# Index heads of a two-block transformer kernel: the two 128-column score products become one 256-column product, and half of the read-out moves from ScalarE to VectorE

## The reference, cut to what matters

```python
s_idx = relu(einsum('bqhd,bkd->bqhk', q_idx, k_idx) * IDX_DIM ** -0.5)   # 8 heads, IDX_DIM 64
score = einsum('bqhk,bqh->bqk', s_idx, w)           # w = w_idx * 8 ** -0.5
score = where(causal, score, -1e30)
_, sel = top_k(score, topk)                         # topk = 64 of 256 keys
```

## Time and profile before

| quantity | value |
|---|---|
| median of the runs | 1114.24 us |
| the profiled execution's own time | 1114.35 us |
| its span, first to last instruction | 1112.5 us |
| busy, TensorE / weight loads | 1106.8 us (99%) / 941.2 us (85%) |
| busy, VectorE / ScalarE / GpSimd | 790.6 us (71%) / 621.2 us (56%) / 58.0 us (5%) |
| mean granted clock of TensorE | 1.000 |

### The profile page before, as it was taken

One profiled execution on the slowest core, in us unless ns is written; L12 is line 12 of the kernel. 1 busy time (PEld: TensorE's weight loads), 2 busy tenths in 40 slices (PEclk: granted clock), 3 DMA queues, 4 the chain that ended last, 5 costly groups with the idle time before them and its releaser, 6 DMA issues.

```text
span 1112.5 us, 14865 instructions
## 1 busy us (share of the span) xinstructions
PE 1106.8 (99%) x5830; PEld 941.2 (85%) x5830; DVE 790.6 (71%) x1136; ACT 621.2 (56%) x825; POOL 58.0 (5%) x105
## 2 busy tenths in 40 slices
PE   9999999999999999999999999999999999999998
PEld 8888888888888888888888888888877788888887
DVE  6777754667987677775477787557898786777752
ACT  6556542677656456554356556337787854656530
POOL 1000000100000000000000000011343000000000
PEclk9999999999999999999999999999999999999999
DMA  9755565654454665555565555557643455555541
GB/s 317 252 190 189 189 246 190 211 162 141 165 195 157 203 189 190 189 189 189 191 206 190 189 189 189 189 154 255 224 150 122 149 181 164 191 188 194 192 179 38
DMA packets 142581, 208.02 MB, mean 187 GB/s; under 512 B 9296, under 2 KB 100584, under 8 KB 142512
## 3 DMA queue, kind: packets, MB, share of 16 engines
q1 hardware_dynamic: 139408, 198.07, 52.7%
q0 software_dynamic: 3088, 9.00, 2.4%
q10 hardware_dynamic: 16, 0.00, 0.0%
HBM read 205.98 MB, written 2.65 MB: 188 GB/s over the span
## 4 chain that ended last, share of the span: by engine, by line
PE 98%; ACT 1%; DMA 0%; issue 0%; DVE 0%; SPq 0%; ACTq 0%; DVEq 0%
PE banks L1810 28%; PE banks L1696 16%; PE banks L1698 16%; PE banks L1697 16%; PE banks L1807 14%; PE banks L1768 1%; PE banks L2046 1%; PE banks L1718 1%; PE banks L1983 1%; DMA raw<-in_ffn_w_gate 0%; PE banks L2076 0%; PE banks L2073 0%; PE banks L2142 0%; PE banks L2016 0%; PE banks L2019 0%
## 5 line engine op out<-in xcount | busy, mean ns | idle before, releaser
L1143 DVE TENSOR_TENSOR w_lo<-raw,w_hi 128x2048 fp32r<-128x2048 f32 x186 | 422.7, 2275 | 167.8 <-ACT w_hi L752 167.5
L752 ACT ACTIVATE w_hi<-raw 128x2048 fp32r<-128x2048 f32 x186 | 352.2, 1897 | 111.8 <-PE banks L1698 108.2
L1810 PE MATMUL banks<-xT,w_hi 128*128 128x512 f32 x1344 | 314.5, 390 | 0.0
L1810 PEld LDWEIGHTS banks<-xT,w_hi 128*128 128x128 f32 x1344 | 249.2, 188 | 49.7
L1696 PE MATMUL banks<-w_hi,xT 128*128 128x512 f32 (+1 forms) x432 | 170.4, 394 | 0.0
L1807 PEld LDWEIGHTS banks<-xT,w_lo 128*128 128x128 f32 x1344 | 167.4, 191 | 3.4
L1807 PE MATMUL banks<-xT,w_lo 128*128 128x256 f32 x1344 | 169.8, 283 | 0.0
L1698 PE MATMUL banks<-w_hi,xT 128*128 128x512 f32 (+1 forms) x432 | 167.0, 387 | 0.0
L1697 PE MATMUL banks<-w_lo,xT 128*128 128x512 f32 (+1 forms) x432 | 166.7, 386 | 0.0
L1696 PE MATMUL banks<-w_hi,hT_hi 128*128 128x512 f32 x352 | 137.3, 390 | 0.0
L830 ACT ACTIVATE gate<-gate 128x256 f32<-128x256 f32 x84 | 35.1, 418 | 182.5 <-DVE gate L1272 182.5
(11 more groups left out here) (324 smaller groups left out, 900.1 us busy)
## 6 DMA issues: line engine op xcount, KB each, us to landing
raw<-in_ffn_w_gate SPq DMA_DIRECT2D x88, 512.0 KB, 3.7
raw<-in_ffn_w_up SPq DMA_DIRECT2D x88, 512.0 KB, 4.7
raw<-in_ffn_w_down SPq DMA_DIRECT2D x88, 512.0 KB, 4.1
raw<-in_w_in SPq DMA_DIRECT2D x76, 512.0 KB, 4.4
raw<-in_w_out SPq DMA_DIRECT2D x16, 512.0 KB, 4.0
raw<-in_w_branch_moba SPq DMA_DIRECT2D x4, 512.0 KB, 4.4
raw<-in_w_branch_sb SPq DMA_DIRECT2D x4, 512.0 KB, 4.9
raw<-in_w_branch_a SPq DMA_DIRECT2D x4, 512.0 KB, 4.2
```

What stands on the lines that cost most here:

```text
L752: act.activation(w_hi[u % SLOTS][:, 0:n], raw[u % RAWS][:, 0:n], ACT.Copy).then_inc(hi_done, 1)
L1143: dve.tensor_tensor(w_lo[r][:, 0:n], raw[r][:, 0:n], w_hi[u % SLOTS][:, 0:n], ALU.subtract).then_inc(lo_done, 1)
L1810: m = pe.matmul(bank[b + s], mh, xT[:, k].rearrange("p a s -> p (a s)"), start=first, stop=k == KC - 1, skip_group_check=c == 0)
```

## The change

TensorE makes three products for an index head: one of 256 columns over both parts of the operand, with its halves in columns 0 to 127 and 384 to 511, and the pair of 256 columns as before. The two halves now have to be added. ScalarE scales and copies columns 384 to 511 to `soft`, and then does scale and relu for columns 128 to 383. VectorE adds the scaled columns 0 to 127 to the copied half (this is its read of PSUM, which frees the bank), adds the weighted second block to the index, bounds and weights the first block, and adds it to the index. The index heads' reader is now VectorE.

```diff
-            it.reader = "a" if kind in ("IX", "CU") else "d"
+            it.reader = "a" if kind == "CU" else "d"
...
                     if it.ix >= 2:
                         act.wait_ge(indexed, it.ix - 1)
-                    act.activation(soft[it.ix % 2][:], bank[4 + it.i % 2][:, 0:SC], ACT.Relu,
-                                   scale=HD ** -0.5).then_inc(read_a, 1)
+                    S, t = bank[4 + it.i % 2], soft[it.ix % 2]
+                    act.activation(t[:, 0:P], S[:, SC:NB], ACT.Copy, scale=HD ** -0.5)
+                    act.activation(t[:, P:SC], S[:, P:SC], ACT.Relu, scale=HD ** -0.5).then_inc(index_copied, 1)
...
                 def accumulate(it):
                     h = it.what
-                    dve.wait_ge(read_a, it.read)
-                    for tt, c in ((0, slice(0, P)), (1, slice(P, SC))):
-                        wt = ifw[:, 8 * tt + h:8 * tt + h + 1]
-                        src = soft[it.ix % 2][:, c]
-                        if h == 0:
-                            ins = dve.scalar_tensor_tensor(index[:, c], src, wt, causal[:, c], ALU.mult, ALU.add)
-                        else:
-                            ins = dve.scalar_tensor_tensor(index[:, c], src, wt, index[:, c], ALU.mult, ALU.add)
-                    ins.then_inc(indexed, 1)
+                    dve.wait_ge(index_copied, it.ix + 1)
+                    t = soft[it.ix % 2]
+                    before = causal if h == 0 else index
+                    w0, w1 = ifw[:, h:h + 1], ifw[:, 8 + h:9 + h]
+                    dve.scalar_tensor_tensor(t[:, 0:P], bank[4 + it.i % 2][:, 0:P], HD ** -0.5, t[:, 0:P], ALU.mult,
+                                             ALU.add).then_inc(read_d, 1)
+                    dve.scalar_tensor_tensor(index[:, P:SC], t[:, P:SC], w1, before[:, P:SC], ALU.mult, ALU.add)
+                    dve.wait_ge(read_d, it.read)
+                    link(dve.tensor_scalar(t[:, 0:P], t[:, 0:P], 0.0, w0, ALU.max, ALU.mult))
+                    dve.tensor_tensor(index[:, 0:P], t[:, 0:P], before[:, 0:P], ALU.add).then_inc(indexed, 1)
                     dve.wait_ge(indexed, it.ix + 1)
...
-                        return st, ik_twice, ik_rest[:, h % 2, :]
+                        pair = sides[1].rearrange("p j a t -> p (j a) t")[:, 0:2 * (h % 2) + 2:2 * (h % 2) + 1, :]
+                        return st, ik_twice, ik_rest[:, h % 2, :], pair
...
-                    elif it.kind == "SM":
+                    else:
                         st, m1, m2, both = operands(it)
                         pe.matmul(S.rearrange("p (a c) -> p a c", c=P)[:, 0:4:3, :], st[:, 0:P], both[:, :, 0:P],
                                   start=True, stop=True)
                         pe.matmul(S[:, P:SC], st[:, P:SEQ], m1, start=True, stop=False)
                         pe.matmul(S[:, P:SC], st[:, P:SEQ], m2, start=False, stop=True).then_inc(scored, 1)
-                    else:
-                        st, m1, m2 = operands(it)
-                        pe.matmul(S[:, 0:P], st[:, 0:P], m1[:, 0:P], start=True, stop=False)
-                        pe.matmul(S[:, 0:P], st[:, 0:P], m2[:, 0:P], start=False, stop=True)
-                        pe.matmul(S[:, P:SC], st[:, P:SEQ], m1, start=True, stop=False)
-                        pe.matmul(S[:, P:SC], st[:, P:SEQ], m2, start=False, stop=True).then_inc(scored, 1)
```

More of the change, by code:

```diff
@@ L378, in build @@
         side_added = sem("side_added")
+        index_copied = sem("index_copied")
         exped = sem("exped")
```

## The result

The changed kernel takes 1117.27 us (median of 8 runs, 1116.83 to 1117.59) against 1114.26 us (8 runs of the kernel before beside them): 3.0 us slower, ratio 1.0027 with a 95% interval of 1.0018 to 1.0036. The forecast was 1117.1 us.

A forecast was written before the change was run, and what follows sets the result against it. The prediction took TensorE's own stream as the path, with VectorE's added work making TensorE wait. It summed 0.99 + 4 x 0.48 - 0.09 = 2.82 us, giving 1117.1 us, own range 1116.7 to 1118.2 us, overall range 1115.4 to 1118.5 us.

The forecast's parts named there:

- The end: At `fk` 0, after the rest of `dk`: TensorE 2.82 us behind, and everything after it equally late.
- three terms: Lateness at `split_lo` of slot 13, 0.99 us; IX 4 to 7, 1.92 us; slack at `fk` 0, -0.09 us.
- VectorE's price of a head: Four VectorE instructions per index head: 0.21 + 0.40 + 0.32 + 0.33 = 1.26 us, 0.48 us more than before.
- The step on which the size hangs: Slots 12 and 13: IX 1's delay holds ScalarE's `split_hi`, so the pause ends later and VectorE's `split_lo` moves 0.99 us.
- the rival of a cost per head: Rival in the runs with some heads: each changed head costs the same, 3.0 / 8 us; no chance given.
- The lateness behind the pause: Slots 13 to 15: IX 4 to 7 add 1.92 us with no pause left, so VectorE is 2.91 us late.
- TensorE's waits: TensorE waits on VectorE at IX 2 and 3, `fq` 0 and `fk` 0: about 1.2, 1.5 and 1.0 us.
- A rule weighed there: VectorE's add out of PSUM: 62 cycles more fixed cost, 0.065 us, making the forecast 0.4 us later; not adopted.
- its opening: Whole span: TensorE busy 99%, VectorE 71%, so TensorE's own stream is the path and its lost time is not made up.
- its faster rival, 1113.4 us: Index-head stages: VectorE's extra work stays in its pauses and TensorE keeps the 0.88 us saved; chance 0.07.

The follow-up runs named there:

- the read-out alone: Against the changed kernel, four products as before and ScalarE's copy makes zeros, with the new ScalarE and VectorE instructions kept: 1117.18 us.
- the run with the adds first: Against the changed kernel, VectorE's two adds out of PSUM for IX 0 and 1 put ahead of the `split_lo` of slot 11: 1117.33 us.
- The run with the merged product alone: Against the kernel before, product merged but the old read-out kept, so columns 384 to 511 are left out of the index: 1114.32 us against 1114.29.
- both GpSimd versions: Against the changed kernel, GpSimd bounds, weights and adds the first block and `split_hi` moves to slot 11: 1116.17 us; with eight tiles for halves too: 1115.02 us.

## Why the prediction was right

- The end: 2.82 us forecast, 2.88 us at `fk` 0 in the trace, 3.01 us between the medians. That only VectorE's lateness counts, and not the merged product, is shown: the read-out alone loses 2.89 us. That the end agrees to 0.06 us is partly luck, since three terms were each off by about 0.1 us and partly cancel: 0.99 forecast and 1.10 measured up to the `split_lo` of slot 13, 1.92 and 1.79 for IX 4 to 7, and -0.09 for a slack that was not there.
- VectorE's price of a head was 1.26 us from rows, 1.24 measured. Each of the four instructions came within 0.02 us of its row.
- The step on which the size hangs was that VectorE's pause is no free room: 0.99 us forecast at the `split_lo` of slot 13, 1.10 measured; the 0.12 us by which VectorE starts IX 0 late was not foreseen. Moving the `split_hi` gives 1.3 us back, and IX 2 and 3, which lie inside the pause, cost nothing. The heads are not equal, as the rival of a cost per head would have it.
- The lateness behind the pause followed: 2.91 forecast at `norm_heads(0)`, 2.89 measured.
- TensorE's waits: 1.2, 1.5 and 1.0 us forecast. From start to start, less the distance where nothing waits (0.23 us, and 0.12 us within a pair of heads), they are 0.45 + 0.81 = 1.26 us at IX 2 and 3, 1.19 at `fq` 0 and 1.26 at `fk` 0, of which 0.25 was there before. The one at `fq` 0 is shorter because TensorE came to it 793.12 + 0.39 - 792.87 = 0.64 us late, where the text had 0.3: it had saved less than 0.88 us, and the first product after each of the two waits took 0.20 us to the next start (775.62 to 775.82) in place of 0.11. That the waits can be shifted with little change in the time is what the run with the adds first shows.
- A rule weighed there, the Trainium skill, VectorE: DVE Perf Modes, section on the TRN2 errata (a dearer PSUM source), is not borne out: the add out of PSUM took 0.29 us here, the add out of SBUF 0.29.
- What the prediction did not see: its opening, that the path is TensorE's own stream, does not hold in this stage, and its faster rival, 1113.4 us, could not have come about even if VectorE had no added work. TensorE already waited 0.25 us for the rest of `dk`, so it could gain next to nothing here by itself. The run with the merged product alone shows this.

## What to carry to other kernels

An engine that is busy for 99% of the span is not for that reason alone on the path: look for the place where the next engine hands it something, and read the slack there before costing a saving, by the distance from start to start, since printed idle time can hide a wait. A pause of an engine is free room only if what ends it does not depend on the work that you mean to put in front of it. In this stage, waits ahead of the last such handing-over neither added up nor subtracted; only the lateness there counted.

## What the runs showed of the hardware

- GpSimd's add of 128x128 takes 0.46 us alone and 2.0 to 2.6 us beside VectorE's subtraction of 128x2048. The Trainium skill, SBUF — State Buffer, section Who interferes with whom, says that a VectorE instruction with two SBUF inputs contends with a GpSimd instruction that reads SBUF; the traces of both GpSimd versions agree.
- Four products of which two have 128 columns took 0.46 us, three of 256 columns 0.35 us, though the number of columns is the same (768): the gain of the merge is in the count of products, not in columns. Each product has a weight load of its own, and from a head's second load on these start 0.11 to 0.12 us apart in both kernels.
- TensorE started `fk` 0 0.14 to 0.15 us after the printed end of VectorE's last read of the bank (all twelve traces), but `fq` 0 0.06 us after the end of `norm_heads(0)`, which writes SBUF (794.48 to 794.54 in the changed kernel).
